# Two layers of a hybrid decoder on one core: 80 token slots instead of 88, and half of each expert's down products turned round

## The reference, cut to what matters

```python
logits = (xt @ router_w).astype(jnp.float32)
top_val, top_idx = lax.top_k(logits, TOP_K)            # 2 of 8
gates = jax.nn.softmax(top_val, axis=-1)
for e in range(N_EXPERTS):
    y = y + combine[:, e:e + 1] * (silu(xt @ w_gate[e]) * (xt @ w_up[e])) @ w_down[e]
```

## Time and profile before

| | us |
|---|---|
| median of three runs | 1589.67 |
| the profiled execution, first to last instruction | 1591.7 |
| first expert product starts | 637.26 |
| last down product ends | 1576.31 |
| TensorE matmul busy | 1517.8 (95%) |
| TensorE weight load busy | 1330.8 (84%) |
| VectorE busy | 256.7 (16%) |
| ScalarE busy | 179.0 (11%) |
| HBM read | 428.89 MB, 270 GB/s over the span |

### The profile page before, as it was taken

The page is one execution under the profiler, slowest core; times in us unless marked ns, Lnnn a source line. Parts: engine busy times, 40 slices in busy tenths (PEclk is TensorE's granted clock), DMA queues, the critical chain, the costliest instruction groups (busy, mean ns, idle before and its releaser), DMA issues.

```text
span 1591.7 us, 54543 instructions
## 1 busy us (share of the span) xinstructions
PE 1517.8 (95%) x25973; PEld 1330.8 (84%) x25973; DVE 256.7 (16%) x489; ACT 179.0 (11%) x383; POOL 143.6 (9%) x167
## 2 busy tenths in 40 slices
PE   8999999999999999999999999999999999999997
PEld 7787587777687865989999999899999999998996
DVE  3433310000143435000010010010000000000102
ACT  3233120000131322100000000000000000000001
POOL 2243200000022532200000000000000000000000
PEclk9999999999999999999999999999999999999999
DMA  9213244444242245999999999999999999999992
GB/s 335 89 53 133 106 159 159 159 159 146 92 161 106 76 154 229 360 377 376 363 374 376 357 348 376 356 382 369 365 376 366 370 367 369 367 355 373 389 379 88
DMA packets 133612, 433.48 MB, mean 272 GB/s; under 512 B 9082, under 2 KB 33916, under 8 KB 119052
## 3 DMA queue, kind: packets, MB, share of 16 engines
q1 hardware_dynamic: 132384, 427.70, 71.9%
q0 software_dynamic: 672, 2.14, 0.4%
q10 hardware_dynamic: 332, 0.13, 0.0%
HBM read 428.89 MB, written 1.05 MB: 270 GB/s over the span
## 4 chain that ended last, share of the span: by engine, by line
PE 92%; issue 3%; DVE 2%; ACT 1%; POOL 1%; DMA 0%; ACTq 0%; DVEq 0%
PE ps L1133 35%; PE ps L1157 18%; PE ps L982 9%; PE ps L681 8%; PE ps L993 4%; PE ps L844 4%; PE ps L692 3%; PE ps L1190 2%; PE ps L1062 1%; PE ps L801 1%; PE ps L714 1%; PE ps L677 1%; PE ps L811 1%; PE ps L707 1%; PE ps L821 1%
## 5 line engine op out<-in xcount | busy, mean ns | idle before, releaser
L1157 PE MATMUL ps<-LT_sb,ring 128*64 128x88 f32 x5376 | 218.4, 239 | 16.2 <-issue 15.1
L1157 PEld LDWEIGHTS ps<-LT_sb,ring 128*64 128x64 f32 x5376 | 212.0, 137 | 21.7 <-issue 19.4
L1133 PE MATMUL ps<-wpost,ring 128*64 128x88 f32 x5376 | 217.0, 240 | 12.4 <-issue 10.9
L1133 PE MATMUL ps<-AT_sb,ring 128*64 128x88 f32 x5376 | 217.0, 239 | 9.9 <-issue 9.7
L1133 PEld LDWEIGHTS ps<-wpost,ring 128*64 128x64 f32 x5376 | 210.9, 138 | 17.5 <-issue 15.4
L1133 PEld LDWEIGHTS ps<-AT_sb,ring 128*64 128x64 f32 x5376 | 211.7, 138 | 14.6 <-issue 13.9
L982 PEld LDWEIGHTS ps<-hT_sb,ring 128*128 128x128 f32 x768 | 136.0, 190 | 24.6 <-issue 9.1
L982 PE MATMUL ps<-hT_sb,ring 128*128 128x256 f32 (+1 forms) x768 | 155.7, 362 | 0.0
L681 PE MATMUL ps<-hT_sb,ring 128*128 128x256 f32 x576 | 128.2, 380 | 0.0
L681 PEld LDWEIGHTS ps<-hT_sb,ring 128*128 128x128 f32 x576 | 108.1, 190 | 15.0 <-issue 0.5
L1985 POOL TENSOR_SCALAR small<-small 128x1 f32<-128x1 f32 x16 | 3.9, 241 | 1203.3 <-ACT late L1513 933.6
(11 more groups left out here) (284 smaller groups left out, 1156.5 us busy)
## 6 DMA issues: line engine op xcount, KB each, us to landing
ring<-in_moe_w_gate SPq DMA_DIRECT2D x84, 1024.0 KB, 8.4
ring<-in_moe_w_up SPq DMA_DIRECT2D x84, 1024.0 KB, 8.0
ring<-in_moe_w_down SPq DMA_DIRECT2D x84, 1024.0 KB, 8.2
late<-in_moe_w_up SPq DMA_DIRECT2D x28, 1024.0 KB, 8.5
late<-in_moe_w_gate SPq DMA_DIRECT2D x28, 1024.0 KB, 7.7
late<-in_moe_w_down SPq DMA_DIRECT2D x28, 1024.0 KB, 8.0
ring<-in_ffn_w_gate SPq DMA_DIRECT2D x11, 1024.0 KB, 5.4
ring<-in_ffn_w_up SPq DMA_DIRECT2D x11, 1024.0 KB, 8.1
```

The source lines that it names most:

```text
L1133: ins = mm(o[lo:lo + P // 2, :], pairs[:, m % 2, lo:lo + P // 2], xgT[e % 2][:, k, :], start=(k == 0 and m % 4 == 0), stop=(k == KD - 1), ...
L1157: ins = mm(o[lo:lo + P // 2, :], d[:, i, m * P + lo:m * P + lo + P // 2], moe_hid[:, 2 * j + i, :], start=(first and m % 4 == 0), stop=las ...
```

## The change

SLOTS goes from 88 to 80, and a fourth round is allowed for. In chunks 2 and 3 of each expert (`BY_TOKEN = 2`) the down products are turned round, in `m_down_by_token`: 128 x 80 of `moe_hid` stands, and 512 columns of the down weights move, so that a unit is 4 calls instead of 32. Their sums go to banks 6 and 7, slots by features. What chunks 0 and 1 gave is copied and transposed into these banks ahead of g3, as plain matmuls with the identity that start the sums to which chunks 2 and 3 add; so the copy, the transposes and `yT_ps` at the expert's end go. The turn marks stay at 8 behind each 256, and the first and third call of each turned unit get marks too. `UNIT_TURN` is dealt out by a table of times for the calls (`CALL_US`) instead of by turns: the 320 units fall due evenly from the first mark to 20 us before the last unit is used. The diff's core (`pe_order`'s new field `how`, the wider `max_val` and the one more compare for the rounds are left out):

```diff
-SLOTS = 88
+SLOTS = 80
-TURN_MARKS = (8,)
-TURNS_AHEAD = 3
-UNIT_CALLS = 32
+TURN_MARK = 8
+LEAD = 20.0
+BY_TOKEN = 2
+TILE_CALLS = 32
+TOKEN_CALLS = 4
+TOKEN_MARKS = (0, 2)
+CALL_US = {"tile": 0.069, "token": 0.853, "gather": 0.042, "oh": 0.07, "y": 0.25, "s": 0.215}
...
-            + [tiles("u", e, 0)] + once(e, e - 1, "y", 8, 2, 8)
+            + [tiles("u", e, 0)]
...
-            + [tiles("u", e, 2), tiles("g", e, 3), tiles("d", e, 2), tiles("u", e, 3)]
+            + [tiles("u", e, 2)] + once(True, e, "y", 8, 4, 8)
+            + [tiles("g", e, 3), tiles("d", e, 2), tiles("u", e, 3)]
...
+    end = used_us[-1] - LEAD
+    for i in range(issues):
+        due = turn_us[0] + (end - turn_us[0]) * i / (issues - 1)
+        turn = next(n for n, us in enumerate(turn_us) if us >= due) + 1
+        unit_turn.append(max(free_at[i], turn))
...
-                    ins = nc.tensor.transpose(bank(6 + m // 4)[0:SLOTS, m % 4 * P:(m % 4 + 1) * P], yT[:, m, :], ident)
+                    ins = mm(bank(6 + m // 4)[0:SLOTS, m % 4 * P:(m % 4 + 1) * P], yT[:, m, :], ident,
+                             start=(m % 4 == 0), stop=False, skip_group_check=True)
...
+            def m_down_by_token(r, e, c):
+                pe.wait_ge(mhid_ready, per_round(r, MOE_CH * e + c + 1, N_CHUNK))
+                call = 0
+                for j in units_of(c, None):
+                    n = UNITS["d", e, c, j]
+                    landed(r, n)
+                    d = down_unit(n)
+                    last = c == MOE_CH - 1 and j == MOE_TILES[c] // 2 - 1
+                    for i in range(2):
+                        for hf in range(2):
+                            ins = mm(bank(6 + hf)[0:SLOTS, :], moe_hid[:, 2 * j + i, :], d[:, i, half(hf)],
+                                     start=False, stop=(last and i == 1), skip_group_check=True)
+                            turned(ins, e, f"d{c}", call)
+                            call += 1
+                    ins.then_inc(unit_used, 1)
```

More of the change, by code:

```diff
@@ L102, with unit_calls @@
 FIRST_IN_PAGE = 103
-TURN_MARKS = (8,)
-TURNS_AHEAD = 3
-UNIT_CALLS = 32
+TURN_MARK = 8
[5 more added lines that the diff above has]
+CALL_US = {"tile": 0.069, "token": 0.853, "gather": 0.042, "oh": 0.07, "y": 0.25, "s": 0.215}
 WAITS = {"g0": 5, "u0": 1, "g1": 2, "d0": 2, "u1": 1, "g2": 2, "gather": 2, "d1": 1, "u2": 1, "g3": 2, "d2": 1,
          "u3": 1, "d3": 1, "y": 2, "s0": 1}
+def unit_calls(kind, c):
+    return TOKEN_CALLS if kind == "d" and c >= BY_TOKEN else TILE_CALLS
 def pe_order(e):
     def tiles(kind, owner, c, part=None):
-        calls = UNIT_CALLS * (MOE_TILES[c] // 2)
+        each = unit_calls(kind, c)
+        calls = each * (MOE_TILES[c] // 2)
         first, n = (0, calls) if part is None else (part * calls // 2, calls // 2)
-        return owner, f"{kind}{c}", f"{kind}{c}" if not part else None, first, n, 4, UNIT_CALLS
+        how = "tile" if each == TILE_CALLS else "token"
+        return owner, f"{kind}{c}", f"{kind}{c}" if not part else None, first, n, 4, each, how
     def once(flag, owner, name, n, size, signal_every):
-        return [(owner, name, name, 0, n, size, signal_every)] if flag else []
+        return [(owner, name, name, 0, n, size, signal_every, name)] if flag else []
     def piece(i):
-        return [(e - 1, "s", f"s{i}", 2 * i, 2, 4, 4)] if e else []
+        return [(e - 1, "s", f"s{i}", 2 * i, 2, 4, 4, "s")] if e else []
     more = e < N_EXP - 1
     return ([tiles("g", e, 0)] + ([tiles("d", e - 1, MOE_CH - 1)] if e else once(True, 0, "oh", 2, 2, 2))
-            + [tiles("u", e, 0)] + once(e, e - 1, "y", 8, 2, 8)
+            + [tiles("u", e, 0)]
             + [tiles("g", e, 1, 0)] + piece(0) + [tiles("g", e, 1, 1)] + piece(1)
@@ L142, in page_turns @@
-    passed = sum(m < FIRST_IN_PAGE for m in TURN_MARKS)
+    at, now, marks, turn_us, free_at, used_us = FIRST_IN_PAGE - WAITS["g0"], 0.0, set(), [], [], []
+    pages = 1
     for e in range(N_EXP):
-        for owner, name, waits, first, calls, size, signal_every in pe_order(e):
+        for owner, name, waits, first, calls, size, signal_every, how in pe_order(e):
             at += WAITS.get(waits, 0)
             for i in range(first, first + calls):
+                if how in ("tile", "token") and i % signal_every == 0:
+                    used_us.append(now)
@@ L147, in page_turns @@
                 at += size
-                if signal_every == UNIT_CALLS and i % UNIT_CALLS == 0:
-                    used_at.append(len(turns))
+                now += CALL_US[how]
                 has_signal = i % signal_every == signal_every - 1
[L151 to L155, removed]
@@ L156, in page_turns @@
-    issues = ROUND_UNITS - N_UNIT
-    unit_turn = [max(free_at[i], 1 + i * (last - 1) // (issues - 1)) for i in range(issues)]
-    assert all(unit_turn[i] <= used_at[N_UNIT + i] - TURNS_AHEAD for i in range(issues))
-    return turns, unit_turn
+                if has_signal and how in ("tile", "token"):
+                    free_at.append(len(turn_us) + 1)
+                turned = at >= pages * PAGE + TURN_MARK
+                if not has_signal and (turned or how == "token" and i % signal_every in TOKEN_MARKS):
+                    marks.add((owner, name, i))
+                    turn_us.append(now)
+                    pages += turned
@@ L408, in build @@
             sem(n) for n in ("msg_ready", "mhid_ready", "y_act", "y_dve", "scatter_ps"))
-        yT_act, yT_dve, yT_ps = (sem(n) for n in ("yT_act", "yT_dve", "yT_ps"))
+        yT_act, yT_dve = (sem(n) for n in ("yT_act", "yT_dve"))
         page_turn = sem("page_turn")
@@ L604, in _ @@
             sp_.wait_ge(rounds_ready, 1)
-            rounds = sp_.value_load(rounds_i[0:1, 0:1], min_val=1, max_val=3)
+            rounds = sp_.value_load(rounds_i[0:1, 0:1], min_val=1, max_val=MAX_ROUNDS)
             with sp_.If(rounds > 1):
@@ L1120, in m_in @@
                 b = 0 if kind == "g" else 2
-                call = UNIT_CALLS * units_of(c, part)[0]
+                call = TILE_CALLS * units_of(c, part)[0]
                 for j in units_of(c, part):
@@ L1152, in m_down @@
                     for i in range(2):
-                        first, last = c == 0 and j == 0 and i == 0, c == MOE_CH - 1 and j == MOE_TILES[c] // 2 - 1 and i == 1
+                        first, last = c == 0 and j == 0 and i == 0, c == BY_TOKEN - 1 and j == MOE_TILES[c] // 2 - 1 and i == 1
                         for m in range(KD):
@@ L1208, in _ @@
             pe.wait_ge(rounds_ready, 1)
-            rounds = pe.value_load(rounds_i[0:1, 0:1], min_val=1, max_val=3)
+            rounds = pe.value_load(rounds_i[0:1, 0:1], min_val=1, max_val=MAX_ROUNDS)
             with pe.Fori(0, rounds) as r:
@@ L1471, in _ @@
             act.wait_ge(rounds_ready, 1)
-            rounds = act.value_load(rounds_i[0:1, 0:1], min_val=1, max_val=3)
+            rounds = act.value_load(rounds_i[0:1, 0:1], min_val=1, max_val=MAX_ROUNDS)
             def onehotT_copy(r, e):
@@ L1882, in _ @@
             step(V.tensor_scalar(cgt, cmax, float(ROUND_LIMITS[0]), None, ALU.is_gt),
-                 V.tensor_scalar(ctwo, cmax, float(ROUND_LIMITS[1]), 1.0, ALU.is_gt, ALU.add))
-            V.tensor_tensor(rounds_i[:, :], cgt, ctwo, ALU.add).then_inc(rounds_ready, 1)
+                 V.tensor_scalar(ctwo, cmax, float(ROUND_LIMITS[1]), 1.0, ALU.is_gt, ALU.add),
+                 V.tensor_scalar(cthree, cmax, float(ROUND_LIMITS[2]), None, ALU.is_gt))
+            V.scalar_tensor_tensor(rounds_i[:, :], cgt, cthree, ctwo, ALU.add, ALU.add).then_inc(rounds_ready, 1)
             dve.wait_ge(rounds_ready, 1)
-            rounds = dve.value_load(rounds_i[0:1, 0:1], min_val=1, max_val=3)
+            rounds = dve.value_load(rounds_i[0:1, 0:1], min_val=1, max_val=MAX_ROUNDS)
             dve.wait_ge(route_exp, 1)
@@ L1933, in _ @@
                     if e:
-                        yT_copy(r, e - 1)
+                        y_copy(r, e - 1)
                     m_hidden(r, e, 0)
                     if e:
-                        y_copy(r, e - 1)
                         accumulate(r, e - 1, 0, 0)
```

36 lines of the change are left out of this document (17 added, 19 removed).

## The result

The changed kernel takes 1597.64 us at the median (1590.66 to 1605.72, seven runs), the kernel before 1589.67 (1582.15 to 1591.37, seven runs). The ratio is 1.0055, 95% interval 1.0035 to 1.0075: 0.55% slower, 8 us, where 12.4 us faster was forecast. The time lies in the range given; the sign is wrong. The rival in which the fetch decides had been priced at 1600.

What follows compares the result with a forecast made beforehand. TensorE and DMA were both near their limits, with TensorE pausing for code fetches delayed by queued weights. Terms -61.9 + 45.6 + 5.7 - 1.1 - 0.7 gave -12.4 us: 1579.3 profiled, 1577 median; range 1553 to 1605.

Steps and rivals of the forecast that it cites:

- The rival in which the fetch decides: Tile pages: unchanged fetch time returns savings as pauses; +22 us, 1611 at worst, 1600 at two thirds; chance 0.33.
- part 6: Instruction fetches on TensorE: fewer, shorter pages with smaller loads ahead; pause total kept at 60 us, so 0.
- Part 1: Tile units on TensorE: 8 columns fewer save 0.215 us a unit over 288 units, -61.9 us.
- Part 2: Turned down products on TensorE: 48 units at 3.43 us instead of 2.48, +45.6 us.
- Part 3: Transposes as plain products on TensorE: 1.72 us each, eight times, +5.7 us.
- Part 4: Gathers on TensorE: fewer columns save 0.15 us, seven times, -1.1 us; scatters 0.
- Part 5: The kernel's end: the copy and its two gaps go, -0.7 us.
- Parts 7 and 8: Loads still land in time, cost 0; VectorE and ScalarE work under 1 us on the path, 0.
- over 75 us of "issue": Sign of the fetch rival: TensorE's "issue" waits before the expert products, against about 46 us forecast.

Runs made afterwards that it cites:

- the finer loads: Each unit loaded by smaller DMAs: 80 slots without turned products, halves 1590.56 us, quarters 1591.93 us; changed kernel, quarters 1622.37 us.
- run 6: Kernel before with the turn mark at 136 instead of 8 instructions behind each page's start: 1689.63 us (1.063).
- run 7: Kernel before with 80 slots, marks at 8 and 136 of each page and loads one at a time: 1600.77 us (1.0064).
- run 10: Kernel before with 80 slots, no turned products, each unit loaded by four DMAs of 256 KB: 1591.93 us (1.0012).
- run 1: Kernel before with each unit from the 17th on loading a quarter of its columns: 1521.08 us (0.958).
- run 3: Kernel before with 80 slots and nothing else changed: 1582.69 us (0.9957).
- run 2: Changed kernel with each unit from the 17th on loading a quarter of its columns: 1515.39 us (0.954).

## Why the prediction was wrong

It named the bound rightly. "Issue" is the page of code that is not there, loads make it late, TensorE never waits for a landing: the quarter loads, the later mark and the fetches' packets show it. It then summed as if TensorE's own work were the path and the pauses a fixed sum on top. That is the step that failed, part 6, "I take the total as it is": two effects of opposite sign were set equal without a reason. That 1597.64 us lies inside the stated 1553 to 1605 is owed to the width that the rivals gave the range, not to the sum. By parts:

- Part 1, tiles, -61.9: 18,432 records 3.31 ns closer are -61.0. Right.
- Part 2, turned units, +45.6: 48 x (3.47 - 2.42) = +50.4 by the quarter loads, where a tile unit without pauses is 64 x 37.86 ns = 2.42 us. I had taken 60 us of pauses out of the mean of before, where the loads cost it 71.9.
- Part 3, transposes, +5.7: 8 x 1.90 - 8.1 = +7.1. Inside the stage it is +8.2 against a forecast of +6.8, since the last transposes before (1.06 us) stood behind it.
- Part 4, gathers, -1.1: 1.83 us for 1.99, seven times, -1.1. Right.
- Not in the sum: the switches between 128 x 64 and 128 x 80 operands around 16 turned stretches. The starts in the changed kernel with quarter loads show them: the first turned record starts 162 ns (median) behind a tile record where the next tile record would start after 35, and the tile record behind a stretch starts after 522 ns instead of 429, together 0.2 us a stretch, some 3 us. What the pair of quarter loads leaves over in the stage, -1.2 - (-61.0 + 50.4 + 8.2 - 1.1) = +2.3 us, agrees, as a little of it is already in the 3.47.
- Part 5, the end, -0.7: from the last down product to the end 1.8 us less, the 0.7 and the 1.06 of the transposes that went from there and stand in part 3. Right.
- Part 6, fetches, 0: loads at full size cost 80.3 us instead of 71.9, +8.4. There were 20 fetches fewer and still more pause.
- Parts 7 and 8: right; no wait of TensorE for a landing in either trace.

The stage was forecast at -61.9 + 45.6 + 6.8 - 1.1 = -10.6 and came at +7.2: 9.4 of the 17.8 between are prices of TensorE (parts 2 and 3 and the switches), 8.4 are pauses. With the prices right and part 6 as it stood, the forecast would have been -1.2 - 1.8 = -3 us, "no change"; only part 6 makes it slower.

The fetch rival had the mechanism: "each page that pauses gives back the whole 0.43 us by which it got shorter". 80 slots alone show it at its purest, 57 of 68 us back, with the fetch's packet starting as late as before. That its 1600 lies so near the measured 1597.64 is luck in part: it had +22 us of pauses on -12.4 of prices, and measured are +8.4 on -3. Nor did its sign show, over 75 us of "issue": there are 58.5, since the turned products take up part of what the narrower tiles give back. The number that should have decided stood in part 6's own rows: two loads per page of 5.42 us, at a DMA share of 1.00, in a kernel in which 150 of 170 turns issue two. Behind two loads the next page's fetch sets the length, and less work in the page does not bring it sooner.

Turning costs 18 us more in the stage than 80 slots alone because its 70 us in TensorE's price take only 121.6 - 71.1 = 50 out of the pauses. Why the other 71 us of pauses did not give way is not shown. It may lie in the unevenness: when a tile stretch gives up loads to a turned stretch, more pages stand behind one load (37 against 20), and such a page lasts 4.72 us for half the bytes of those of 5.54. That reading is argued from page lengths; the finer loads that should have tested it brought a cost of their own, so it stays open. Open too is why one turned chunk costs next to nothing and two cost 16 us by the ratios (18 in the stage).

## What to carry to other kernels

When long straight code runs beside saturated loads, look at what a page of code and its pause last together, grouped by the loads issued in it, before pricing a cheaper instruction: if that sum is set by the loads, the saving comes back as pause. Run both versions once with a quarter of the load bytes; the pair shows each kernel's own price in one number, and would have shown here that the change was worth 1 us in the stage. Where the trace lists DMA packets, look when the packets of code start and end: a pause that ends a fixed time behind one of them (1.4 us here) is a late fetch. Of the placements tried here, loads right behind the page's turn (runs 6 and 7) and in large pieces (run 10) did best.

## What was not expected of the hardware

- A fetch of 16 KB of code lasts 1.0 us whether the loads are full or a quarter; it is its start that slips, from the page's boundary to some 2.7 us behind it (before, and run 1). TensorE goes on 1.4 us after the fetch has ended.
- The place of a load within the page of code matters more than any operation of this change: 128 instructions later, +97 us in 939 (run 6).
- 256 KB DMAs move 361 GB/s at full share of the 16 engines where 1 MB ones move 381 (runs 10 and 3).
- Going over from column-halved tiles to whole ones and back costs about 0.2 us a stretch over the operations' own price (162 ns for 35 and 522 for 429, run 2).
- 8 of 88 columns fewer give 3.31 of 38.29 ns a record: 0.414 ns a column, which makes 36.4 ns for 88, and 1.9 ns of a record are not columns (an estimate from the two).
